# A 31-tap convolution shared between VectorE and a ScalarE-GpSimd pair, three-pass input projections, and a first expert selection in halves

## The reference

```python
h = rmsnorm(x, norm1_g)
z = h @ w_in + b_in                                  # 5376 columns
glu_val, glu_gate, q, k, v, g_conv, g_attn = split(z, [1024, 2048, 3072, 3200, 3328, 4352])
u = glu_val * sigmoid(glu_gate)
y = depthwise_conv(pad(u, 30), conv_w) + conv_b      # 31 taps per channel, causal
y = silu(layernorm(y)) @ w_conv_out
q, k = rope(q), rope(k)                              # 16 query heads, 2 key heads of 64
a = windowed_attention(q, k, v, sinks) @ w_attn_o    # softmax over 128 back, a sink per head
x = x + (sigmoid(g_conv) * y + sigmoid(g_attn) * a) @ w_out
h2 = rmsnorm(x, norm2_g)
q = (h2 @ w_peer_q).reshape(256, 8, 2, 128)          # 8 expert heads, 2 halves
s_top, i_top = top_k(q . sub_keys, 16)               # for each half, of 128 keys
best, pos = top_k(all 16 x 16 sums, 16)              # 16 experts for each token and head
x = x + sum over 128 experts of softmax(best) * gelu(u_emb[e] . h2) * v_emb[e]
```

## Time and profile before

| | us |
|---|---|
| median of three runs | 1613.77 |
| the profiled execution, whole | 1610.89 |
| its span, first to last instruction | 1609.1 |
| TensorE busy | 1452.7 (90%) |
| VectorE busy | 992.1 (62%) |
| ScalarE busy | 621.8 (39%) |
| GpSimd busy | 316.4 (20%) |
| mean DMA rate | 266 GB/s |

### The profile page before, as it was taken

How to read it: one execution, slowest core, us unless ns; L and a number is a source line. 1 busy time by engine, 2 the same in 40 slices (tenths; PEclk the granted TensorE clock), 3 DMA queues, 4 the chain that set the end, 5 groups by cost and what they waited for, 6 DMA issues and landing times.

```text
span 1609.1 us, 16567 instructions
## 1 busy us (share of the span) xinstructions
PE 1452.7 (90%) x5958; PEld 997.1 (62%) x5958; DVE 992.1 (62%) x1967; ACT 621.8 (39%) x1294; POOL 316.4 (20%) x298
## 2 busy tenths in 40 slices
PE   7999998989987777788887779989999999999998
PEld 6768897745533333333333237767888879878886
DVE  6995775767767677776675543336555455565553
ACT  2014672233333334433333224454444335544442
POOL 2000000344443444445444410400000000000000
PEclk9999999999999999999999999999999999999999
DMA  7445654999999999999999955413554444155451
GB/s 298 154 163 150 132 230 150 420 413 419 419 421 420 420 417 410 419 391 420 412 411 420 420 234 193 162 54 111 203 186 180 170 170 158 76 199 196 171 197 65
DMA packets 52210, 428.56 MB, mean 266 GB/s; under 512 B 6696, under 2 KB 6840, under 8 KB 10144
## 3 DMA queue, kind: packets, MB, share of 16 engines
q0 software_dynamic: 40464, 279.18, 43.4%
q1 hardware_dynamic: 11664, 148.33, 24.3%
HBM read 422.49 MB, written 4.98 MB: 266 GB/s over the span
## 4 chain that ended last, share of the span: by engine, by line
PE 65%; DMA 20%; DVE 8%; ACT 4%; issue 2%; POOL 1%; SPq 0%; DVEq 0%; ACTq 0%; POOLq 0%
DMA pool<-uv,experts 19%; PE psum L765 17%; PE psum L1146 11%; PE psum L898 11%; PE psum L899 10%; PE psum L900 10%; PE psum L799 3%; DVE pool L2071 3%; PE psum L845 2%; DMA ring<-stream 1%; DVE ring_lo L1722 1%; ACT diag L1558 1%; ACT xn L1238 1%; POOL pool L716 1%; ACT coef L1552 1%
## 5 line engine op out<-in xcount | busy, mean ns | idle before, releaser
L1146 PE MATMUL psum<-pool,diag 128*128 128x512 f32 x1024 | 478.9, 618 | 113.0 <-ACT diag L1558 113.0
L1146 PEld LDWEIGHTS psum<-pool,diag 128*128 128x128 f32 x1024 | 193.4, 196 | 389.7 <-issue 209.3
L2071 DVE CUSTOM_DVE_ANT_0 pool<-pool,xn 128x1024 f32<-128x1024 f32 x256 | 313.4, 1226 | 195.9 <-DMA pool<-uv,experts 193.1
L716 POOL DMA_INDIRECT pool<-uv,experts x256 | 285.2, 1114 | 501.4 <-PE psum L1146 355.3
L1722 DVE TENSOR_TENSOR ring_lo<-ring,w_hi 128x2048 fp32r<-128x2048 f32 x76 | 173.9, 2291 | 114.0 <-ACT w_hi L1330 114.0
L1548 ACT ACTIVATE acts<-dots 128x2 f32<-128x2 f32 x128 | 26.0, 203 | 374.5 <-DVE dots L2071 374.4
L1330 ACT ACTIVATE w_hi<-ring 128x2048 fp32r<-128x2048 f32 x76 | 144.4, 1908 | 65.6 <-PE psum L900 37.3
L898 PE MATMUL psum<-w_hi,h_hi 128*128 128x512 f32 x400 | 161.3, 403 | 2.5 <-DVE ring_lo L1722 0.9
L765 PE MATMUL psum<-hT,ring 128*128 128x256 f32 (+1 forms) x768 | 159.7, 369 | 3.0 <-DMA ring<-stream 1.2
L899 PE MATMUL psum<-ring_lo,h_hi 128*128 128x512 f32 x400 | 157.1, 393 | 0.0
L900 PE MATMUL psum<-w_hi,h_lo 128*128 128x512 f32 x400 | 156.1, 390 | 0.0
(11 more groups left out here) (277 smaller groups left out, 1913.4 us busy)
## 6 DMA issues: line engine op xcount, KB each, us to landing
ring<-stream SPq DMA_DIRECT2D x65, 2048.0 KB, 7.6
pool<-uv,experts POOLq DMA_INDIRECT x256, 12.7
ring<-stream SPq DMA_DIRECT2D x3, 1024.0 KB
t_scratch<-tab POOLq DMA_DIRECT2D x1, 2048.0 KB, 56.9
rpb_scratch<-tab POOLq DMA_DIRECT2D x1, 1792.0 KB, 23.3
ring<-stream SPq DMA_DIRECT2D x1, 1792.0 KB, 7.2
row<-rows POOLq DMA_DIRECT2D x1, 1672.0 KB, 11.6
ring<-stream SPq DMA_DIRECT2D x1, 1664.0 KB
```

Source lines behind the costliest of these rows:

```text
L716: gp.indirect_dma_start(out=gath[:, n % NROWS, :], out_offset=None, in_=uv, in_offset=bass.IndirectOffsetOnAxis(ap=experts[:, n:n + 1], ax ...
L1146: last = nc.tensor.matmul(psum[:, RB + half, :], diag[:, n % NDIAG, :], gath[:, n % NROWS, D + 512 * half:D + 512 * half + 512], start=k = ...
L2071: ins = V.tensor_tensor_reduce(out=row_u, in0=row_u, in1=xn[:, n // SLOTS, :], scale=1.0, scalar=0.0, op0=ALU.mult, op1=ALU.add, accum_out ...
```

## The change

Three things are changed.

- **Convolution.** VectorE keeps channel blocks 0 to 3 (124 taps) and accumulates them in PSUM banks 6 and 7; ScalarE copies them to `y` later (`conv_copy`). For blocks 4 to 7, ScalarE makes each product (tap weight times shifted input, 128x256) into one of four buffers and GpSimd adds it to `y` in SBUF (124 instructions on each). ScalarE's products are placed by constants between its other duties, and each waits for a free buffer. TensorE's first values of `att1` wait for the copies, and `conv_sum` waits for GpSimd's last add.
- **Projections.** `glu` chunks 1 to 3, `q1` and `kv1` are made in three passes: eleven parts of 128x2048 are split by ScalarE and VectorE, and the normed input is split once (`n_hi`, `n_lo`).
- **Chain.** For token tile 0 the sum of squares, the norm, the transposes, the query and the scores of head 0 go in two halves. The last `wout` work moves behind them on TensorE. The expert numbers come in two sets of eight ranks; GpSimd starts after the first, and its first four gathers do not wait for the last `wout` fill.

The diff, cut to its core:

```diff
-TAPS_AFTER_GLU = (13, 15, 15, 15, 15, 15, 15, 84)
-TAPS_AFTER_ROPE = 12
-TAPS_IN_HEAD = 4
+TAPS_AFTER_GLU = (3, 7, 7, 7, 7, 7, 7, 4)
+TAPS_BEFORE_KV, TAPS_AFTER_KV = 22, 30
+TAPS_IN_HEAD = 0
+VECTOR_BLOCKS = 4
+POOL_TAPS = [(m + j, w) for m in range(VECTOR_BLOCKS, KD, 2) for w in range(TAPS) for j in range(2)]
+NPRODUCTS = 4
+PRODUCTS_AFTER_GLU = {5: 6, 6: 7, 7: 7}
+PRODUCTS_AFTER_EVICTION = 7
+PRODUCTS_AFTER_GATE, PRODUCTS_AFTER_TURN, PRODUCTS_IN_HEAD = 4, 3, 2
...
+ROWS_BELOW_WEIGHTS = 4
...
+            for n, (m, w) in enumerate(POOL_TAPS):
+                gp.wait_ge(product_ready, n + 1)
+                if w:
+                    nc.gpsimd.tensor_tensor(y[:, m, :], y[:, m, :], products[:, n % NPRODUCTS, :], ALU.add
+                                            ).then_inc(product_added, 1)
+                else:
+                    nc.gpsimd.tensor_copy(y[:, m, :], products[:, n % NPRODUCTS, :]).then_inc(product_added, 1)
+                gp.wait_ge(product_added, n)
...
-            gp.wait_ge(bank_filled, FILL_NO["wout", 1, 1] + 1)
             for n in range(NT * SLOTS):
-                if n % TOPK == 0:
+                if n == ROWS_BELOW_WEIGHTS:
+                    gp.wait_ge(bank_filled, FILL_NO["wout", 1, 1] + 1)
+                if n == 0:
+                    gp.wait_ge(first_ranks, 1)
+                elif n == TOPK // 2:
+                    gp.wait_ge(selected, 1)
...
+                    elif h == 0:
+                        pe.wait_ge(conv_copied, VECTOR_BLOCKS // 2)
...
-            feature_major("glu", 4)
-            token_major_chunks("q1", 2, hT)
-            token_major_chunks("kv1", 1, hT, 256)
+            feature_major("glu", 1)
+            pe.wait_ge(normed_split, 1)
+            normed_halves = (n_hi, n_lo)
+            for q in range(EARLY_GLU, EARLY_Q):
+                split_feature_major(-2, q, normed_halves)
+            for i in range(2):
+                for t in range(NT):
+                    tile_products(("q1", i), -2, EARLY_Q + 2 * i, normed_halves, t)
...
+            def first_query_and_scores():
+
+                w = wait_chunk(pe, ("pq", 0))[:, 0:4096].rearrange("p (k n) -> p k n", k=KD)
+                query = [psum[:, RB, 0:P], begin(("pqt", 0, 0))[:, P:2 * P]]
+
+                def part(c, ks):
+                    for k in ks:
+                        last = nc.tensor.matmul(query[c], w[:, k, P * c:P * c + P], hT[:, k, tile128(0)],
+                                                start=k == 0, stop=k == KD - 1)
+                    return last
+
+                wait_emptied(pe, ("N2", 0, 0))
+                part(0, range(4))
+                wait_emptied(pe, ("N2", 0, 1))
+                part(0, range(4, KD)).then_inc(half_filled, 1)
+                part(1, range(4))
+                score = begin(("sct", 0, 0))
+                pe.wait_ge(query_half_copied, 1)
+                nc.tensor.matmul(psum[:, RB + 1, 0:NKEYS], qpT[:, 0, 0, tile128(0)], keys[:, 0, :], start=True, stop=True
+                                 ).then_inc(half_filled, 1)
+                part(1, range(4, KD)).then_inc(bank_filled, 1)
+                wait_emptied(pe, ("pqt", 0, 0))
+                nc.tensor.matmul(score[:, NKEYS:2 * NKEYS], qpT[:, 0, 1, tile128(0)], keys[:, 1, :], start=True, stop=True
+                                 ).then_inc(bank_filled, 1)
+
             out_projection(0, 0)
             out_projection(1, 0)
-            out_projection(0, 1)
+            other = begin(("wout", 0, 1))
+            half_products(-1, WOUT, (merged_hi, merged_lo), other, 1)
             pe.wait_ge(keys_landed, 16)
-            tile_transposes("N2", 0, xn[:, 0, :])
-            wait_tile("N2", 0)
-            tile_query(0, 0)
-            tile_scores(0, 0)
+            pe.wait_ge(front_normed, 1)
+            transposes(("N2", 0, 0), [xn[:, 0, P * k:P * k + P] for k in range(4)])
+            pe.wait_ge(xn_ready, xn_before["N2"] + 1)
+            transposes(("N2", 0, 1), [xn[:, 0, P * k:P * k + P] for k in range(4, KD)])
+            first_query_and_scores()
+            half_products(-1, WOUT + 1, (merged_hi, merged_lo), other, 1)
+            out_projection(1, 1)
             tile_query(1, 0)
-            out_projection(1, 1)
             tile_scores(1, 0)
...
+            def conv_products(count):
+
+                for n in range(products_made[0], min(products_made[0] + count, len(POOL_TAPS))):
+                    m, w = POOL_TAPS[n]
+                    products_made[0] = n + 1
+                    if w == 0:
+                        wait_emptied(act, ("glu", m // 2, m % 2))
+                    if n >= NPRODUCTS:
+                        act.wait_ge(product_added, n - NPRODUCTS + 1)
+                    out, src, tap = products[:, n % NPRODUCTS, :], u[:, m, w:w + S], conv_w[:, m, w:w + 1]
+                    if w:
+                        ins = nc.scalar.activation(out, src, ACT.Copy, scale=tap)
+                    else:
+                        ins = nc.scalar.activation(out, src, ACT.Identity, bias=par_("conv_b")[:, m:m + 1], scale=tap)
+                    ins.then_inc(product_ready, 1)
...
+            nc.scalar.activation(n_hi[:, :, :], hT[:, :, :], ACT.Copy).then_inc(normed_high, 1)
...
+                split_high(-2, m + 1)
...
+                conv_products(PRODUCTS_AFTER_GLU.get(m, 0))
+            split_high(-2, KD + 1)
             for i in range(2):
                 for t in range(NT):
                     empty(("q1", i, t), qkv[:, t, 512 * i:512 * i + 512])
+                    conv_products(PRODUCTS_AFTER_EVICTION)
+                if i == 0:
+                    split_high(-2, EARLY_KV)
             for t in range(NT):
                 empty(("kv1", 0, t), qkv[:, t, 1024:1280], lambda b: b[:, 0:256])
+                conv_products(PRODUCTS_AFTER_GATE)
+            def conv_copy(pair):
+                act.wait_ge(conv_ready, 2 * pair + 2)
+                nc.scalar.activation(y[:, 2 * pair:2 * pair + 2, :],
+                                     psum[:, RB + pair, :].rearrange("p (m s) -> p m s", m=2), ACT.Copy
+                                     ).then_inc(conv_copied, 1)
+
+            conv_copy(0)
             for n in range(GATES_FIRST):
                 gate_copy(n)
+                conv_products(PRODUCTS_AFTER_GATE)
             for t in range(NT):
                 for hf in range(2):
+                    conv_products(PRODUCTS_AFTER_TURN)
...
+            conv_copy(1)
...
+            def first_root():
+                load_roots()
+                wait_emptied(act, ("wout", 0, 0))
+                step(nc.scalar.activation(xn[:, 0, 0:512], x[:, 0, 0:512], ACT.Square, accum_out=ssq_half[:, 0:1]))
+                step(nc.scalar.activation(half_bias, ssq_half[:, 0:1], ACT.Identity, bias=eps, scale=1.0 / D))
+                wait_emptied(act, ("wout", 1, 0))
+                step(nc.scalar.activation(xn[:, 0, 512:D], x[:, 0, 512:D], ACT.Square, accum_out=ssq_half[:, 1:2]))
+                nc.scalar.activation(rstd[:, 0:1], ssq_half[:, 1:2], ACT.Sqrt, bias=half_bias, scale=1.0 / D
+                                     ).then_inc(root_ready, 1)
...
+                    acc = psum[:, RB + m // 2, S * (m % 2):S * (m % 2) + S]
...
+                        ins = V.scalar_tensor_tensor(acc, src, tap, acc, ALU.mult, ALU.add)
...
+                split_low(-2, m + 1)
                 conv_taps(TAPS_AFTER_GLU[m])
+            split_low(-2, KD + 1)
+            conv_taps(TAPS_BEFORE_KV)
+            split_low(-2, EARLY_KV)
+            conv_taps(TAPS_AFTER_KV)
...
-            conv_taps(TAPS_AFTER_ROPE)
+            conv_taps(CONV_TAPS)
+
             def conv_sum():
-                conv_taps(CONV_TAPS)
-                dve.wait_ge(conv_ready, KD)
+                dve.wait_ge(conv_copied, VECTOR_BLOCKS // 2)
+                dve.wait_ge(product_added, len(POOL_TAPS))
...
+            def first_norm():
+
+                dve.wait_ge(root_ready, roots_before["N2"] + 1)
+                r = rstd[:, 0:1]
+                link(V.reciprocal(r, r))
+                gain = row_("norm2")
+                V.scalar_tensor_tensor(xn[:, 0, 0:512], x[:, 0, 0:512], r, gain[:, 0:512], ALU.mult, ALU.mult
+                                       ).then_inc(front_normed, 1)
+                V.scalar_tensor_tensor(xn[:, 0, 512:D], x[:, 0, 512:D], r, gain[:, 512:D], ALU.mult, ALU.mult
+                                       ).then_inc(xn_ready, 1)
...
+                ranks(0).then_inc(first_ranks, 1)
+                link(V.match_replace(first_cand, best[:, 0:8], first_cand, -3.0e38))
+                ranks(8).then_inc(selected, 1)
...
-            second_norm(0)
+            first_norm()
+            first_selection()
             add_tile(0, 1)
-            for k in range(SELECT_STEPS):
-                select_step(0, k)
```

More of the change, by code:

```diff
@@ L256, in part_end @@
         return (name, i, side)
+    if name == "kv1":
+        return (name, i, 1)
     if layer < 0 or q < DOWN:
@@ L364, in build @@
```

(19 more changed lines are left out.)

96 lines of the change are left out of this document (85 added, 11 removed).

## The result

The changed kernel takes 1648.26 us (median of four runs, 1643.01 to 1650.99) against 1613.01 of the kernel before on the same chip: a ratio of 1.0225, 95% interval 1.0209 to 1.0241. The profiled execution has a span of 1646.4 us, 37.3 more than before. The forecast was 1607.0, in a range of 1594 to 1624.

What follows compares the result with a forecast made beforehand. TensorE was taken as the main bound up to the attention, the gathers from 277.79 us on. The sum 14.5 - 4.8 - 3.0 - 4.9 + 5.0 = 6.8 us faster gave 1607.0 against 1613.77, range 1594 to 1624.

Steps and rivals of the forecast that it cites:

- The front: Up to the first masked score: 14.5 us gained by the projections, 4.8 lost to ScalarE's products before the attention.
- Exclusion: From 54 us to the attention: GpSimd's adds and VectorE's two-input instructions shut each other out; 12.5 us lost, 1619.5, chance 0.20.
- The add at 0.65: One 128x256 add on GpSimd was taken at 0.65 us, between 0.556 and 1.17.
- just covered on the mean, but not where it is dense: Before the last turned query's eviction: 88 adds take 57 us from about 54, ending at 111.
- The 23 taps behind the rotation: VectorE before the first scores: 9 us of taps from 105, ending near ScalarE's work and costing nothing more.
- The projections in three passes: `glu`, `q1` and `kv1` on TensorE: 14.5 us gained, the sixth gate ending at about 111 instead of 125.7.
- the cover of two blocks: In the `glu` blocks: parts are split two blocks ahead, which covers a lag of some 6 us.
- VectorE's readiness: Before the attention: VectorE reaches the bias at 93 and is ready at 105, 6 us before TensorE.
- Part (b): In the attention: two ScalarE products stand before the next exponentials after odd heads' gates; 0.5 us each, 3.0 us lost.
- Part (c): At the attention's end: the last products delay the sum of `y`, so the division starts at 192.2; 4.9 us lost.
- The chain in halves: Behind the attention: first search 4.9 us sooner, first ranks 2.0, first gather 6.9; a gain of 5 taken.
- The rival of 0.07: In the gathers: the chain's gain is lost and only 2 us arrive, 1610; chance 0.07.

Runs made afterwards that it cites:

- reordered kernel: Half the adds on GpSimd (blocks 2 and 3), then products regrouped around the splits and taps moved behind the rotation, against the changed kernel: 1609.45 us, ratio 0.9984.
- adds paused: Changed kernel with GpSimd's two stores ahead of the 97th add, and GpSimd held before its 49th add until the bias addition is done: 1631.67 us, ratio 1.012.
- adds one by one: Changed kernel with the stores ahead of the 97th add, and no add begun before the last is complete: 1638.04 us, ratio 1.016.
- two blocks: Changed kernel with GpSimd adding only blocks 2 and 3 (62 products); VectorE keeps the other blocks: 1609.1 us, ratio 0.9983.

## Why the prediction was wrong, point by point

Four terms failed. The front (up to the first masked score) was put at 9.7 us sooner, 14.5 less 4.8, and came 10.5 later: 20.2 off, the largest miss, since the adds on GpSimd and VectorE's wait for them were priced too low. The stores behind the adds, 18.6, had no term. The attention cost 8.6 for 7.9, and of the 5 us of the chain next to nothing arrived.

**A queue that was not gone through (18.6 us).** The largest term of the loss is in no sentence of the prediction. It costed the adds by duration and by who waits for them, but not what stands behind them on GpSimd: two stores, on which SyncE and through it the weights depend. In the trace of before they were plain to see at 143.79 and 145.48. By moving these two instructions 17 us came back.

**Exclusion was the right rival, with too small a price.** It was given 12.5 us and a chance of 0.20, as a sum of both engines' work: as if they took turns. They did take turns from 113.71 on (1.16 to 1.29 for 0.75), but only after the adds had first shut VectorE out over 20 instructions. Its argument against, the taps beside GpSimd's instruction at 31.0, held for a single instruction of 56 rows and was carried too far. The rule of the Trainium skill (SBUF — State Buffer, "Who interferes with whom"), that such a pair shuts each other out for the whole instruction, agrees: in the reordered kernel an add of 0.73 took 3.31 us across the bias addition. The section also says that the order of issue decides who is shut out. That did not hold here: in seven kernels adds that were issued behind VectorE's instruction went ahead of it, for 13.2 to 21.5 us. But the wait was not the whole price: freed of it, in the kernel with the adds paused, the first score came no sooner than 138.45.

**The add at 0.65 was 0.70, and the sum was made as a mean.** 0.70 agrees with the estimate of 0.69 in the prediction. But "just covered on the mean, but not where it is dense" was said and not costed. The row of 124 adds, with its evictions behind it, was a second bound up to the first score, hidden behind VectorE's wait: the score came at 142.50 where 121 to 123 were forecast, and with VectorE freed still at 138.45, within 1.4 us of the last add. That the row is the bound is shown by the two kernels in which VectorE is free (adds paused, adds one by one); for the kernel after it follows from them. The 23 taps behind the rotation, said to cost nothing, ended with the first score at 142.50 there, where TensorE had begun the scores at 139.35: about 3 us at most.

**The projections in three passes were right in their mechanism.** `glu` filled 5.65 us apart (5.6). PSUM taps were 0.39 apart (0.40), and 0.52 where one block stood alone. The sixth gate ended at 116.2 and not 111, since ScalarE's lag used up the cover of two blocks and TensorE waited 2.82 us; in the reordered kernels, without the lag, it ended at 110.5 and 110.3. From the first chunk on that is 13.4 us sooner than before: the gain of 14.5 was nearly right. VectorE's readiness was not. It came to the sinks at 99.63 and not 93, since it had waited 10.1 us for ScalarE, 8.7 of them for high halves, where some 3 were put. With the same taps ahead and the rotation undisturbed it was ready at 114.0 (two blocks) where 105 was forecast; 106.1 came only with 16 taps fewer ahead of the bias.

**In and behind the attention.** Part (b) was put at 3.0 us; a pair of heads grew by 0.76, which is 5.3 in seven. Part (c) was put at 4.9; the sum of `y` waited for the last adds and the division for it, and 3.3 are left for that. Together 8.6 against 7.9: the sum is right by luck, its parts are off by 2.3 and 1.6 in opposite directions.

**The chain in halves: the steps right, the arrival wrong.** 4.9 and 2.0 us were foreseen, 4.9 and 2.1 came. But "between 2 and 6.9 arrive; I take 5" was taken from the first gather. The prediction itself had the row that speaks against it: the ninth gather waits for TensorE, behind tile 1's queries, and tile 1's norm is not made sooner. In the kernel after (against the sum of squares) and with the chain alone it moved by 0.9 us or less. The rival of 0.07 was the true case for this term, with about 1 instead of 2.

**The sum as it was**: front 10.47, attention 8.59, stores 18.55, chain -0.3, together 37.3. The stretch of the stores took 0.55 us more than before even with the stores early, so 18.0 of its 18.55 are theirs.

## What to carry to other kernels

When work is put on an engine, go through everything that stands behind it in that engine's program, down to its DMA issues, and whoever waits for those. Order a long row of GpSimd instructions away from VectorE's work on SBUF: with half of the adds, the stores no longer held up by them, and the rotation in their break, the change brought 0.5% where it had cost 2.25%. A step that comes sooner on a chain is worth what the next join allows; look at the other arm of the join first.

## What the runs showed of the hardware

- A one-input VectorE instruction of 16 elements a row took 13.3 to 21.6 us instead of 0.17 while GpSimd added back to back, the next add begun before the last had ended; with each add held until the last was complete such instructions waited 0.2 and 0.5 us. It is not shown what decides in a row without gaps.
- Once VectorE had come in, both engines took turns, beside adds as close as before: 1.16 to 1.29 for 0.75 on VectorE, 1.24 for 0.73 on GpSimd. VectorE's taps that accumulate in PSUM kept their 0.39 beside the densest adds.
- A waiting TensorE lost its clock as well: in 120 to 140 us of after it was busy for 8.74 of 20 us at a granted 0.60 (window of that stretch: length, busy time of PE, PEld, DVE, ACT and POOL, clock, DMA share, GB/s).

```profile
120.00:140.00 20.00, 8.74 (x40) 7.89 (x41) 19.86 (x31) 9.44 (x20) 15.88 (x17) 0.60 0.00 0
```
